# DeltaNet block inversion: turning the inverse in 32x32 blocks on VectorE instead of by TensorE products and a ScalarE copy

## Chip, cores and metric

One core of one Trainium2 chip. The metric is device time in microseconds (us) of one execution, as the median of several runs. TensorE (PE), VectorE (DVE), ScalarE (ACT), GpSimd (POOL) and the DMA queues (SP) run beside each other and meet at semaphores.

## What is computed

A two-layer backbone over 256 context and 256 latent tokens of 1024 channels. Each layer is a half-step SwiGLU feed-forward network, a token mixer, and another half-step feed-forward network; the first mixer is a state-space scan (S5), the second a gated DeltaNet. The change lies in the DeltaNet mixer. For each of 8 heads and 2 scan directions the reference takes chunks of tokens and solves with a unit lower triangular matrix:

```python
decay = jnp.exp(jnp.where(incl, gcum[..., :, None] - gcum[..., None, :], -jnp.inf))
a_mat = jnp.where(strict, jnp.einsum('bhncd,bhnsd->bhncs', k_beta, k) * decay, 0.0)
lhs = a_mat + jnp.eye(GDN_CHUNK, dtype=a_mat.dtype)
u_val = lax.linalg.triangular_solve(lhs, v * beta[..., None], left_side=True, lower=True)
w_key = lax.linalg.triangular_solve(lhs, k_beta * jnp.exp(gcum)[..., None], left_side=True, lower=True)
```

The rest of the mixer (projections, a convolution of five taps over q, k and v, SiLU, norms, the scan over chunks, an output projection) and the networks around it are untouched.

## The kernel before

The tokens are cut into 4 chunks (NCH) of 128, and the kernel forms the inverse of each chunk's triangular matrix, for both directions d = 0, 1. The 128 rows are two halves i of 64 (SUB), which lie on partitions 0 to 63 and 64 to 127. All tiles of the inversion (X, BT, BB, NN) hold 4 chunks of 64 columns for each direction, 128x256 fp32 in all.

`invert(h)` exists three times, for TensorE (line 1747), ScalarE (line 1982) and VectorE (line 2142), each engine walking through the same 10 rounds, in each round first d = 0, then d = 1. After a round's last product TensorE counts up "prod"; VectorE waits for it, evaluates and counts up "evd"; ScalarE, in the rounds listed in `ACT_ROUNDS` (line 1514), copies another bank and counts up "eva". TensorE waits for both before the next round of that direction (lines 1756 to 1758).

- Rounds 0 to 3 build the inverse of the 16x16 diagonal blocks by repeated squaring: X is multiplied up, BB and BT are the power and its transpose. The last addition to X is in round 3 (line 2153).
- Rounds 4 and 5 join pairs of blocks of 16 into blocks of 32, rounds 6 and 7 those of 32 into 64. In round 4 or 6 TensorE turns X by products with an identity (line 1775, 8 products for each direction) and then multiplies NN with half of X's columns (line 1778, 8 products). ScalarE copies the turned X to BT (line 1992), VectorE masks the other product to BB (line 2155). In round 5 or 7 TensorE multiplies BT and BB (line 1783) and VectorE adds the result to half of X's columns (line 2160).
- Rounds 8 and 9 join the two halves of 64 (lines 1785 to 1792, 2162, 2164). Round 8 turns X on half of the partitions and copies it to BT on ScalarE.

Each small product is written through `small`, so the trace has all of them under line 1639; each counts there as two weight loads and two matmuls, and a group of 8 as 16 records. "PS<-consts,X" is a turning product, "PS<-X,NN" the product of round 4 or 6, "PS<-BB,BT" that of round 5, 7 or 9.

Between the rounds the engines also work for the next head. VectorE issues one tap of the next head's key or value convolution (lines 2066, 2069) behind the rounds of `CONV_AFTER` (line 1515): (0,0), (0,1), (1,0), (1,1), (2,0), (3,1), (4,0), (5,1), (6,0), (7,1), written as (round, direction). The last head has none. Each tap but the first waits for the tap before it. ScalarE splits a weight block behind round 2 and runs the SiLU of the next head's keys behind round 4 and of its values behind round 8 (lines 1994 to 1997); the keys' SiLU needs the fifth tap, issued behind (2,0). After round 7 ScalarE copies X to XX (line 2001). Then comes `chain(h)`, the scan over the chunks, with the projection products of head h + 2 (line 1652) put between its steps, and `prepare(h + 1)`.

The order of all of this is the order in which each engine's program is written; there is no planner. All engines' work in this stage is written out, head by head.

```python
            def small(pe, dst, lhsT, rhs, at_row, at_col):

                return pe.matmul(dst, lhsT, rhs, start=True, stop=True, tile_position=(SUB * at_row, SUB * at_col))
```

Of the kernel before, what the change touches and what calls it, by code (L numbers as in the profile page):

```python
# [47 lines left out]
H = 8  # L48
CH = 128
NCH = T // CH  # L50
SUB = CH // 2
# [72 lines left out]
def program(nc, A, out):  # L124

    ctx = ExitStack()
    with ctx:
# [1292 lines left out]
        def glu_pe(pe):  # L1420
# [11 lines left out]
            with pe.Fori(1, KT // 2) as i:  # L1432
# [54 lines left out]

        PER = {"pc": 3, "zr": 1, "conv": 15, "silu": 4, "square": 2, "ss": 1, "norms": 4, "kroot": 1,
# [4 lines left out]
        gs_ = {n: sem("g_" + n) for n in PER}  # L1493
# [17 lines left out]
            ins.then_inc(gs_[name], 1)  # L1511

        ORDER = [(0, 1, 2, 3), (1, 0, 3, 2)]
        ACT_ROUNDS = [0, 1, 2, 4, 6, 8]
        CONV_AFTER = [(0, 0), (0, 1), (1, 0), (1, 1), (2, 0), (3, 1), (4, 0), (5, 1), (6, 0), (7, 1)]
        BESIDE = 2

# [119 lines left out]
        def small(pe, dst, lhsT, rhs, at_row, at_col):  # L1637

            return pe.matmul(dst, lhsT, rhs, start=True, stop=True, tile_position=(SUB * at_row, SUB * at_col))  # L1639
# [17 lines left out]
        def gdn_pe(pe):  # L1657
# [89 lines left out]
            def invert(h):  # L1747
                for rnd in range(10):
                    for d in range(2):
                        banks = ((1, 3, 6), (4, 5, 7))[d]  # L1750
                        if rnd == 0:
                            need(pe, "bt", h, d + 1)
                            need(pe, "bb", h, d + 1)
                            need(pe, "nn", h, d + 1)
                        else:
                            need(pe, "evd", h, 2 * (rnd - 1) + d + 1)
                            if rnd - 1 in ACT_ROUNDS:
                                need(pe, "eva", h, 2 * ACT_ROUNDS.index(rnd - 1) + d + 1)
                            if rnd == 1:
                                need(pe, "x0", h, d + 1)  # L1760
                                if d == 0:
                                    need(pe, "nn", h, 3)
                                else:
                                    need(pe, "kd", h, 2)
                        todo = [[(BB, BT), (BT, BB)], [(BB, X), (BB, BT), (BT, BB)], [(BB, X), (BT, BB)], [(BB, X)]]
                        level = (rnd - 4) // 2
                        if rnd < 4:
                            for (lt, rt), bank in zip(todo[rnd], banks):
                                for c in range(NCH):
                                    for i in range(2):  # L1770
                                        last = small(pe, PS[sub(i), bank, c * SUB:(c + 1) * SUB], lt[sub(i), d, c, :], rt[sub(i), d, c, :], i, i)
                        elif rnd in (4, 6):
                            for c in range(NCH):
                                for i in range(2):
                                    small(pe, PS[sub(i), banks[0], c * SUB:(c + 1) * SUB], X[sub(i), d, c, :], eye_sub[sub(i), :], i, i)
                            for c in range(NCH):
                                for i in range(2):
                                    last = small(pe, PS[sub(i), banks[1], c * SUB // 2:(c + 1) * SUB // 2], NN[sub(i), d, c, :],
                                                 half_columns(X[sub(i), d, c, :], d, level), i, i)
                        elif rnd in (5, 7):  # L1780
                            for c in range(NCH):
                                for i in range(2):
                                    last = small(pe, PS[sub(i), banks[2], c * SUB // 2:(c + 1) * SUB // 2], BT[sub(i), d, c, :],
                                                 BB[sub(i), d, c, 0:SUB // 2], i, i)
                        elif rnd == 8:
                            for c in range(NCH):
                                small(pe, PS[sub(d), banks[0], c * SUB:(c + 1) * SUB], X[sub(d), d, c, :], eye_sub[sub(d), :], d, d)
                                last = small(pe, PS[sub(d), banks[1], c * SUB:(c + 1) * SUB], NNo[sub(1 - d), c, :],
                                             X[sub(1 - d), d, c, :], 1 - d, d)
                        else:  # L1790
                            for c in range(NCH):
                                last = small(pe, PS[sub(d), banks[2], c * SUB:(c + 1) * SUB], BT[sub(d), d, c, :], BB[sub(d), d, c, :], d, d)
                        told(last, "prod")
# [100 lines left out]
        def gdn_act(act):  # L1894
# [87 lines left out]
            def invert(h):  # L1982
                for n, rnd in enumerate(ACT_ROUNDS):
                    for d in range(2):
                        banks = ((1, 3, 6), (4, 5, 7))[d]
                        need(act, "prod", h, 2 * rnd + d + 1)
                        if rnd == 0:
                            need(act, "x0", h, d + 1)
                        copies = {0: [(BT, 0)], 1: [(BT, 1), (BB, 2)], 2: [(BB, 1)]}.get(rnd, [(BT, 0)])
                        rows_ = sub(d) if rnd == 8 else slice(0, P)  # L1990
                        for t, b in copies:
                            last = act.activation(t[rows_, d, :, :].rearrange("p c t -> p (c t)"), PS[rows_, banks[b], 0:NCH * SUB], ACT.Copy)
                        told(last, "eva")
                    if rnd == 2 and h + 1 < H:
                        split_half(1, u0 + h + 2, 0)
                    if rnd in (4, 8) and h + 1 < H:
                        silu(h + 1, (rnd - 4) // 4)
                for d in range(2):
                    need(act, "evd", h, 15 + d)
                    for i in range(2):  # L2000
                        last = act.activation(XX[sub(i), d, :, sub(i)], X[sub(i), d, :, :], ACT.Copy)
                    told(last, "xx")
# [50 lines left out]
        def gdn_dve(dve):  # L2053
# [88 lines left out]
            def invert(h):  # L2142
                ahead = list(conv_steps(h + 1))[:10] if h + 1 < H else []
                for rnd in range(10):
                    for d in range(2):
                        banks = ((1, 3, 6), (4, 5, 7))[d]
                        level = (rnd - 4) // 2
                        need(dve, "prod", h, 2 * rnd + d + 1)
                        if rnd == 0:
                            last = dve.tensor_copy(BB[:, d, :, :].rearrange("p c t -> p (c t)"), PS[:, banks[1], 0:NCH * SUB])  # L2150
                        elif rnd < 4:
                            xd = X[:, d, :, :].rearrange("p c t -> p (c t)")
                            last = dve.tensor_tensor(xd, xd, PS[:, banks[0], 0:NCH * SUB], ALU.add)
                        elif rnd in (4, 6):
                            last = dve.tensor_tensor(BB[:, d, :, 0:SUB // 2],
                                                     PS[:, banks[1], 0:NCH * SUB // 2].rearrange("p (c t) -> p c t", c=NCH),
                                                     join(level, d).unsqueeze(1).to_broadcast([P, NCH, SUB // 2]), ALU.mult)
                        elif rnd in (5, 7):
                            xd = half_columns(X[:, d, :, :].rearrange("p c t -> p (c t)"), d, level)
                            last = dve.tensor_tensor(xd, xd, PS[:, banks[2], 0:NCH * SUB // 2].rearrange("p (b j) -> p b j", j=C16 << level), ALU.add)  # L2160
                        elif rnd == 8:
                            last = dve.tensor_copy(BB[sub(d), d, :, :].rearrange("p c t -> p (c t)"), PS[sub(d), banks[1], 0:NCH * SUB])
                        else:
                            last = dve.tensor_copy(XX[sub(d), d, :, sub(1 - d)],
                                                   PS[sub(d), banks[2], 0:NCH * SUB].rearrange("p (c t) -> p c t", c=NCH))
                        told(last, "evd")
                        if ahead and (rnd, d) in CONV_AFTER:
                            conv(h + 1, *ahead.pop(0))

# [370 lines left out]
```

## Time and profile before

| | |
|---|---|
| median of 3 runs | 2112.87 us (2112.18 to 2113.4) |
| the profiled execution, its own time | 2116.53 us |
| its span, first to last instruction | 2114.7 us |
| mean granted TensorE clock | 0.971 |
| TensorE busy | 1974.8 us, 93% |
| TensorE weight loads | 1671.6 us, 79% |
| VectorE busy | 1482.6 us, 70% |
| ScalarE busy | 707.2 us, 33% |
| GpSimd busy | 589.1 us, 28% |

Busy time is the time in which at least one instruction of the engine runs. Matmuls overlap, so a busy TensorE isn't TensorE at its peak. The DeltaNet heads lie between about 1500 and 1856 us of the span. A line of the trace names the source line, the operation, the tile written, the tiles read, and the shape; the bracket at its end is idle time of that engine just before it, and who ended it. Times on the left of a timeline count from the span's start.

### The profile page before, as it was taken

To read this page: it belongs to the slowest core of one execution; us is meant where nothing else is said; L and a number is where in the kernel's file an instruction comes from. 1 tells how busy PE (TensorE), PEld (TensorE's weight loads), DVE (VectorE), ACT (ScalarE), POOL (GpSimd) and SP (SyncE) were. 2 spreads that over 40 slices of the span, in tenths; PEclk is the share of its full clock that TensorE was granted. 3 is DMA by queue.
4 is the path that set the end of the run, shared out by engine and by line. 5 is a ranking of instruction groups with operands and counts; after the bars stand their busy time and mean duration, and the time that the engine had idled before them with its cause. 6 is when DMAs were issued, how large, how long until landed. Compare 5 with 4: busy or idle time off the path is not lost.

```text
span 2114.7 us, 37558 instructions
## 1 busy us (share of the span) xinstructions
PE 1974.8 (93%) x14838; PEld 1671.6 (79%) x14838; DVE 1482.6 (70%) x2273; ACT 707.2 (33%) x1126; POOL 589.1 (28%) x465
## 2 busy tenths in 40 slices
PE   3999999997998999999989999998999999879997
PEld 0778778776986788888768888886888998779996
DVE  8968768757735985858989486358577777655555
ACT  2322222224333421222243122225455555426332
POOL 2245575553922120212412021140000000022113
PEclk8999999998999999999999999998999999989999
DMA  8365665655734354644425353222111111014553
GB/s 324 130 243 197 202 223 202 211 178 204 295 120 138 120 179 139 216 142 154 175 100 192 135 178 139 95 85 64 42 45 50 50 42 61 23 60 161 179 178 98
DMA packets 85633, 305.04 MB, mean 144 GB/s; under 512 B 9856, under 2 KB 21632, under 8 KB 76032
## 3 DMA queue, kind: packets, MB, share of 16 engines
q1 hardware_dynamic: 80896, 285.41, 39.5%
q0 software_dynamic: 2304, 9.44, 1.1%
q10 hardware_dynamic: 2304, 8.39, 1.0%
q8 instruction: 92, 1.51, 0.3%
q14 instruction: 37, 0.30, 0.0%
HBM read 275.94 MB, written 27.26 MB: 143 GB/s over the span
## 4 chain that ended last, share of the span: by engine, by line
PE 82%; DVE 9%; ACT 3%; issue 2%; POOL 2%; DVEq 1%; DMA 1%; SPq 0%; ACTq 0%; POOLq 0%
PE PS L228 41%; PE PS L219 6%; PE PS L221 6%; PE PS L220 6%; PE PS L1639 6%; PE PS L1652 6%; PE PS L1236 1%; DVE wlo L264 1%; PE PS L620 1%; DVE rstd L386 1%; PE PS L1071 1%; POOL hidl L603 1%; PE PS L1198 1%; PE PS L1218 1%; PE PS L1045 1%
## 5 line engine op out<-in xcount | busy, mean ns | idle before, releaser
L264 DVE TENSOR_TENSOR wlo<-raw,whi 128x1024 fp32r<-128x1024 f32 x314 | 479.0, 1566 | 80.9 <-ACT whi L258 79.2
L228 PE MATMUL PS<-hh,whi 128*128 128x512 f32 (+1 forms) x1536 | 443.9, 371 | 37.2 <-DVE hl L407 30.0
L228 PE MATMUL PS<-hl,whi 128*128 128x512 f32 (+1 forms) x1536 | 440.1, 368 | 0.0
L228 PE MATMUL PS<-hh,wlo 128*128 128x512 f32 (+1 forms) x1536 | 439.3, 368 | 0.0
L258 ACT ACTIVATE whi<-raw 128x1024 fp32r<-128x1024 f32 x300 | 301.3, 1052 | 277.6 <-PE PS L221 246.0
L228 PEld LDWEIGHTS PS<-hh,whi 128*128 128x128 f32 x1536 | 278.0, 191 | 92.4 <-issue 37.6
L228 PEld LDWEIGHTS PS<-hl,whi 128*128 128x128 f32 x1536 | 280.3, 191 | 47.2
L228 PEld LDWEIGHTS PS<-hh,wlo 128*128 128x128 f32 x1536 | 280.2, 191 | 47.1
L601 POOL CAST hidh<-gt 128x512 f32 (+2 forms) x88 | 62.0, 704 | 860.7 <-DVE gt L549 860.7
L219 PE MATMUL PS<-hidh,whi 128*128 128x512 f32 (+1 forms) x704 | 259.3, 368 | 12.7 <-POOL hidl L603 10.0
L221 PE MATMUL PS<-hidh,wlo 128*128 128x512 f32 (+1 forms) x704 | 256.6, 365 | 0.0
L220 PE MATMUL PS<-hidl,whi 128*128 128x512 f32 (+1 forms) x704 | 256.6, 364 | 0.0
L520 ACT ACTIVATE gt<-PS 128x512 f32<-128x512 f32 (+1 forms) x88 | 47.9, 544 | 570.8 <-PE PS L228 570.7
L649 DVE CUSTOM_DVE_ANT_0 junk<-modw,cb,modb 128x1024 f32<-128x1024 f32 x160 | 216.9, 1356 | 4.3
L586 DVE SCALAR_TENSOR_TENSOR x<-PS,hg,x 128x256 f32<-128x256 f32 (+1 forms) x176 | 77.9, 478 | 154.6 <-PE PS L221 152.0
L219 PEld LDWEIGHTS PS<-hidh,whi 128*128 128x128 f32 x704 | 133.7, 190 | 37.9 <-POOL hidl L603 12.7
L603 POOL TENSOR_TENSOR hidl<-gt,hidh 128x512 f32 (+2 forms) x88 | 157.6, 1791 | 12.6 <-POOL hidh L601 10.8
L549 DVE TENSOR_TENSOR gt<-gt,PS 128x512 f32<-128x512 f32 (+1 forms) x88 | 54.7, 621 | 138.4 <-ACT gt L520 135.5
L221 PEld LDWEIGHTS PS<-hidh,wlo 128*128 128x128 f32 x704 | 133.5, 190 | 21.0
L220 PEld LDWEIGHTS PS<-hidl,whi 128*128 128x128 f32 x704 | 133.7, 190 | 20.1
L2279 POOL TENSOR_TENSOR X<-BT,consts 128x256 f32<-128x256 f32 x16 | 13.6, 847 | 344.6 <-DVE BT L2122 344.6
L1652 PE MATMUL PS<-hh,whi 128*128 128x512 f32 (+1 forms) x256 | 72.6, 366 | 7.8 <-DVE hl L407 7.6
(336 smaller groups left out, 2755.5 us busy)
## 6 DMA issues: line engine op xcount, KB each, us to landing
modw<-in_mod_w SPq DMA_DIRECT2D x72, 1024.0 KB, 5.0
raw<-in_w_gdn SPq DMA_DIRECT2D x32, 512.0 KB, 4.1
cxd<-cx POOLq DMA_DIRECT2D x16, 576.0 KB, 3.8
cxS<-cxd SPq DMA_DIRECT2D x8, 1152.0 KB, 6.2
raw<-in_w_f0p0a SPq DMA_DIRECT2D x16, 512.0 KB, 6.9
vwd<-vws ACTq DMA_DIRECT2D x16, 512.0 KB, 6.5
raw<-in_w_f0p1a SPq DMA_DIRECT2D x16, 512.0 KB, 5.6
raw<-in_w_glu SPq DMA_DIRECT2D x16, 512.0 KB, 4.6
```

The costliest lines, as they stand in the source:

```text
L219: pe.matmul(dst, w_h, xh, start=first, stop=False)
L220: pe.matmul(dst, w_h, xl, start=False, stop=False)
L221: return pe.matmul(dst, w_l, xh, start=False, stop=last)
L228: ended = pe.matmul(dst, of[:, slot, c:c + P], moving, start=first and part_ == 0, stop=last and part_ == 2)
L258: act.activation(whi[:, s, c], raw[:, s, c], ACT.Copy).then_inc(whi_ready[half][s], 1)
L264: dve.tensor_tensor(wlo[:, s, c], raw[:, s, c], whi[:, s, c].bitcast(F32), ALU.subtract)\
L586: last = dve.scalar_tensor_tensor(out=xv, in0=pv, scalar=hg[:, layer, n, bass.ds(dt, 1), w:w + 1].rearrange("p a b -> p (a b)"), in1=xv, o ...
L601: pool.tensor_copy(hidh[:, bass.ds(2 * i + s, 1), c0:T], gt[:, s:s + 1, c0:T]).then_inc(hidh_ready[s], 1)
L603: pool.tensor_tensor(hidl[:, bass.ds(2 * i + s, 1), c0:T], gt[:, s:s + 1, c0:T], hidh[:, bass.ds(2 * i + s, 1), c0:T].bitcast(F32), ALU.su ...
L649: dve.tensor_tensor_reduce(out=junk[:, :], in0=modw[:, k % MS, D * j:D * j + D], in1=cb[:, w, :], scale=1.0, scalar=modb[:, layer, a:a + 1 ...
L1639: return pe.matmul(dst, lhsT, rhs, start=True, stop=True, tile_position=(SUB * at_row, SUB * at_col))
L1652: last = pe.matmul(PS[:, 2 * s + i, 0:T - c0], (whi, whi, wlo)[part_][:, s, (2 * k + i) * P:(2 * k + i + 1) * P], (hh, hl, hh)[part_][:, k ...
```

## The change

Rounds 4 and 6 lose their turning products on TensorE and their copies to BT on ScalarE. Behind its additions to X in rounds 3 and 5 VectorE waits for its own result and then turns each 32x32 block of X[:, d] in place of the block, into BT. Round 8 keeps its products and its copy. ScalarE's rounds become 0, 1, 2 and 8, and the SiLU of the next head's keys moves from behind round 4 to behind round 2. The number of "eva" counts of a head drops from 12 to 8.

```diff
-               "ntT": 3, "nn": 3, "bt": 2, "bb": 2, "x0": 2, "xx": 2, "prod": 20, "eva": 12, "evd": 20, "RS": 6, "qS": 4, "r2": 6,
+               "ntT": 3, "nn": 3, "bt": 2, "bb": 2, "x0": 2, "xx": 2, "prod": 20, "eva": 8, "evd": 20, "RS": 6, "qS": 4, "r2": 6,
...
-        ACT_ROUNDS = [0, 1, 2, 4, 6, 8]
+        ACT_ROUNDS = [0, 1, 2, 8]
...
                         elif rnd in (4, 6):
                             for c in range(NCH):
                                 for i in range(2):
-                                    small(pe, PS[sub(i), banks[0], c * SUB:(c + 1) * SUB], X[sub(i), d, c, :], eye_sub[sub(i), :], i, i)
-                            for c in range(NCH):
-                                for i in range(2):
                                     last = small(pe, PS[sub(i), banks[1], c * SUB // 2:(c + 1) * SUB // 2], NN[sub(i), d, c, :],
                                                  half_columns(X[sub(i), d, c, :], d, level), i, i)
...
-                    if rnd in (4, 8) and h + 1 < H:
-                        silu(h + 1, (rnd - 4) // 4)
+                    if rnd in (2, 8) and h + 1 < H:
+                        silu(h + 1, rnd // 8)
...
                         told(last, "evd")
+                        if rnd in (3, 5):
+                            need(dve, "evd", h, 2 * rnd + d + 1)
+                            dve.transpose(BT[:, d, :, :].rearrange("p c t -> p (c t)"), X[:, d, :, :].rearrange("p c t -> p (c t)"))
                         if ahead and (rnd, d) in CONV_AFTER:
                             conv(h + 1, *ahead.pop(0))
```

## Rows read from the trace of the kernel before

**Rows 1.** The page, part 4: shares of the chain that ended last, by engine.

```profile
PE 82%; DVE 9%; ACT 3%; issue 2%; POOL 2%; DVEq 1%; DMA 1%; SPq 0%; ACTq 0%; POOLq 0%
```

**Rows 2.** Stretches: from:to, length, busy us (x records) by engine, clock, DMA.

```profile
1489.40:1494.20 4.80, 2.89 (x23) 2.46 (x23) 4.21 (x16) 4.72 (x11) 0.68 (x1) 1.00 0.00 0
1494.50:1497.50 3.00, 3.00 (x26) 2.67 (x25) 2.37 (x6) 2.75 (x8) 0.73 (x1) 0.50 0.02 5
1553.10:1571.30 18.20, 16.23 (x497) 15.59 (x496) 13.38 (x31) 8.80 (x19) 1.12 (x2) 1.00 0.19 62
1571.30:1602.00 30.70, 30.52 (x242) 27.41 (x240) 23.30 (x64) 16.77 (x43) 1.70 (x2) 1.00 0.11 35
1835.60:1839.00 3.40, 3.40 (x71) 3.40 (x68) 1.04 (x3) 0.77 (x2) 1.12 (x2) 0.50 0.02 5
```

**Rows 3.** Timeline of TensorE's weight loads, head 1, rounds 3 to 9 (start, length).

```profile
1562.04 0.54 PEld L1639 LDWEIGHTS PS<-X,BB 64*64 64x64 f32 x16 [0.24 <-DVE X L2153]
1562.50 0.55 PEld L1639 LDWEIGHTS PS<-consts,X 64*64 64x64 f32 x16
...
1564.36 0.55 PEld L1639 LDWEIGHTS PS<-BB,BT 64*64 64x64 f32 x16
1565.10 0.57 PEld L1639 LDWEIGHTS PS<-BB,BT 64*64 64x64 f32 x16 [0.19 <-DVE BB L2155]
...
1568.19 0.48 PEld L1639 LDWEIGHTS PS<-BB,BT 64*64 64x64 f32 x13 [0.18 <-DVE BB L2155]
...
1570.24 1.00 PEld L1639 LDWEIGHTS PS<-BB,BT 64*64 64x64 f32 x16 [0.44 <-DVE BB L2162]
```

**Rows 4.** Timeline of VectorE, head 1, rounds 2 to 8.

```profile
1561.57 0.82 DVE L2153 TENSOR_TENSOR X<-X,PS 128x256 f32<-128x256 f32 x2
1562.77 0.42 DVE L2153 TENSOR_TENSOR X<-X,PS 128x256 f32<-128x256 f32 x1 [0.38 <-PE PS L1639]
1563.11 0.48 DVE L2066 TENSOR_SCALAR cv<-pv,convw 128x512 f32<-128x512 f32 x1
1563.67 0.29 DVE L2155 TENSOR_TENSOR BB<-PS,consts 128x128 f32<-128x128 f32 x1
1563.88 0.74 DVE L2069 SCALAR_TENSOR_TENSOR cv<-pv,convw,cv 128x512 f32<-128x512 f32 x1
1564.61 0.29 DVE L2155 TENSOR_TENSOR BB<-PS,consts 128x128 f32<-128x128 f32 x1
1565.07 0.29 DVE L2160 TENSOR_TENSOR X<-X,PS 128x128 f32<-128x128 f32 x1 [0.17 <-PE PS L1639]
...
1568.91 0.29 DVE L2160 TENSOR_TENSOR X<-X,PS 128x128 f32<-128x128 f32 x1 [0.47 <-PE PS L1639]
...
1569.78 0.87 DVE L2162 COPY BB<-PS 64x256 f32<-64x256 f32 x2
```

**Rows 5.** Timeline of VectorE, four taps in a row, each waiting for the last.

```profile
1461.21 3.12 DVE L2069 SCALAR_TENSOR_TENSOR ck<-pk,convw,ck 128x512 f32<-128x512 f32 x4
```

**Rows 6.** Timeline of ScalarE, head 1, round 4.

```profile
1564.61 0.38 ACT L1992 ACTIVATE BT<-PS 128x256 f32<-128x256 f32 x1 [0.55 <-PE PS L1639]
1565.01 1.28 ACT L1926 ACT_TABLE_LOAD   x1
```

**Rows 7.** Groups by line and shape in the DeltaNet stage: one group of VectorE.

```profile
L2212 DVE TENSOR_TENSOR oo<-oo 128x256 f32<-128x256 f32 x7 | 3.0, 425 | 0.2
```

**Rows 8.** Timeline of VectorE, head 0: X(3,1) and BB(8,0).

```profile
1513.89 0.42 DVE L2153 TENSOR_TENSOR X<-X,PS 128x256 f32<-128x256 f32 x1 [0.36 <-PE PS L1639]
...
1520.90 0.87 DVE L2162 COPY BB<-PS 64x256 f32<-64x256 f32 x2
```

**Rows 9.** Timeline of VectorE, head 7: X(3,1) and BB(8,0).

```profile
1844.29 0.42 DVE L2153 TENSOR_TENSOR X<-X,PS 128x256 f32<-128x256 f32 x1 [0.36 <-PE PS L1639]
...
1850.91 0.42 DVE L2162 COPY BB<-PS 64x256 f32<-64x256 f32 x1 [0.18 <-PE PS L1639]
```

**Rows 10.** Waits of TensorE from 1500 to 1856 us: total, times, longest.

```profile
PE PS L1639 <- issue: 6.0, 7, 1.3
```

## Prediction

> **What bounds the kernel now.** I read the page's last chain first, to see which engine sets the end; then stretches of one head of the DeltaNet stage, to see whether that holds inside the inversion; then the instructions of TensorE and VectorE there, one by one, because the change moves work between these two. In the chain of the whole run TensorE has 82% and VectorE 9% [rows 1], so TensorE's work normally counts in full. In head 1 the scan after the inversion is TensorE without a hole: 30.52 us busy of 30.70. The inversion before it is not: 16.23 of 18.20, with VectorE busy for 13.38 [rows 2]. Ten rounds go back and forth between the two, with the two directions of the scan taking turns to hide the way.
>
> **The marks of head 1** [rows 3, 4]. A group of 8 small products (16 records) starts 0.47 us after the one before (1562.04, 1562.50). VectorE starts on its result 0.71 to 0.73 us after the group's start (1564.36 to 1565.07, 1562.04 to 1562.77). TensorE starts 0.05 after the end of the VectorE result it waits for (X of round 2 ends at 1561.99, group at 1562.04). On VectorE an instruction that waits for nothing starts 0.08 before its predecessor's end (1562.77 + 0.42 = 1563.19, next at 1563.11). One that waits for its predecessor's own result starts later: four taps in a row take 3.12 us, at 0.74 each 0.79 from start to start, so 0.045 after the end [rows 5, 4].
>
> **What goes from TensorE.** Rounds 4 and 6 lose the transposing products, one group of 0.47 us for each of two directions: 4 groups, 1.87 us a head, 14.9 us in 8 heads. ScalarE loses four copies a head. Of these, the one at 1564.61 ends at 1564.99, later than VectorE's 1564.90, and the group starts at 1565.10 instead of 1564.95 [rows 3, 4, 6]: 0.15 us of waiting that goes, twice a head (round 5 and round 7).
>
> **What comes to VectorE.** After the additions into X of rounds 3 and 5, for each direction, one transposition of 128x256 fp32, with a wait for X's own end: 4 a head, 32 in all. The trace has none. The nearest rows are one pass over 256 columns: 0.42 from SBUF to SBUF [rows 7] and 0.42 with PSUM [rows 4]. The lower bound is the 0.29 of a pass over 128 columns, the upper the 0.74 of one over 512 (as if it needed two passes) [rows 4]. I take 0.42: same columns, type and memory. They cannot save anything by themselves; that is in the TensorE terms.
>
> **The walk through a head, at 0.42.** A tap of the next head's convolution still stands behind each odd round's second direction and each even round's first, and it is now queued behind the transpositions too.
> - X(3,0) (round 3, direction 0) ends at 1562.39; its transposition takes 1562.44 to 1562.86. X(3,1) may start at 1562.77, starts at 1562.78, ends at 1563.20. Nearly free: it fills the 0.38 of idle before it.
> - Transposition 1563.24 to 1563.66, tap to 1564.06, BB(4,0) 1563.98 to 1564.27 (was 1563.67): TensorE needed it at 1564.36 and now starts round 5 at 1564.32. So the products removed bought 0.04 there.
> - Tap to 1564.93, BB(4,1) 1564.85 to 1565.14; round 5's second group at 1565.19, was 1565.10.
> - X(5,0) 1565.06 to 1565.35, transposition to 1565.82; X(5,1) waits for its product: 1565.92 to 1566.21 (0.18 of slack). Transposition to 1566.67, tap to 1567.33, BB(6,0) 1567.25 to 1567.54, tap to 1568.20, BB(6,1) 1568.12 to 1568.41. Round 7 starts at 1567.59, and its second group at 1568.46, was 1568.19.
> - X(7,1) 1569.19 to 1569.48 (was 1568.91), tap to 1570.15, BB(8,0) at 1570.07, was 1569.78. Round 9 waits for that, was 1570.24, now 1570.53.
>
> So a head with taps gets 0.29 us **longer**: 1.87 us leave TensorE, and VectorE's queue, 2.2 us longer (4 x 0.42 and four waits of 0.125), is what is late next. From X(3,1) to BB(8,0) there are 7.01 us in head 1 and in head 0 [rows 4, 8]; heads 2 to 6 run the same instructions in the same order: 7 x 0.29 = +2.0 us. Head 7 has no taps; there the distance is 6.62 [rows 9]. The same walk from 1844.29 without them puts X(7,1) at 1849.05 and BB(8,0) at about 1849.64 instead of 1850.91: -1.3 us. **Sum: +0.7 us.** What follows (ScalarE's copies of X into XX, the scan) hangs on the same marks and moves along.
>
> One more look at the wait. The Trainium skill ("VectorE: DVE Perf Modes", The DRAIN you can't avoid) says that semaphores between chained VectorE operations cost nothing extra. By that, two of the 0.125 us on the path would go, and the sum would be about -1.0 us. The taps' 0.79 against a step of 0.34 without such a wait speaks against it.
>
> **Costed at nothing.** The SiLU of the keys moves on ScalarE from behind round 4 to behind round 2. Its table load of 1.28 [rows 6] and the SiLU, under 1 us, now lie where ScalarE has no copy until round 8, some 4 us later; without that cover it would be up to 2.3 us a head. Its input is the fifth tap, which is issued in round 2. No DMA and no other queue is touched. TensorE's waits for "issue" in these products, 6.0 us in 7 places [rows 10], may move, since the stream loses instructions and those behind get other places: between 0 of them and twice as many, -6 to +6. I take 0.
>
> **Rivals.**
> - **A: TensorE stays the bound, faster.** If VectorE's additions fell in its idle time, all of the 14.9 us would come: 2112.9 - 14.9 = 2098. For it: VectorE is idle 4.8 us of the 18.20 [rows 2]. Against: the idle time lies before round 3's second half and in rounds 0 to 2, not behind the taps, where the queue is closed from 1563.24 to 1565.35. A milder form: the issue waits shrink by over 5 us, giving 2108.
> - **B: the block transposition is slow, slower.** Three of the four lie in the closed queue and the fourth has 0.18 of slack. Each 0.1 us more costs 0.3 us a head, above 0.60 it costs 0.4. From about 0.57 us the kernel is slower by over 0.2%; at 0.74 a head costs 1.4 us: +10 us, 2123.
> - **C: TensorE's clock falls, slower.** The granted clock fell to half (1.2 of 2.4 GHz) after a stretch with 2.89 us busy of 4.80, and at half clock 71 small products take 3.40 us, 0.77 a group instead of 0.47 [rows 2, 3]. The walk leaves TensorE about 55% issuing in rounds 5 to 7. If it falls late in the inversion, the scan begins at half clock: with about 1.7 us of it there, and two groups that take 0.3 longer, 2.3 us a head, +16 us, 2129. Against: TensorE's wait of 1.3 us among these products [rows 10] left the clock at 1.00 in head 1. The Trainium skill ("TensorE: Matmul & The Clock Gate", A second HAM failure mode) says that small idle gaps between groups of products can make the clock swing to and fro; head 1, with clock 1.00 at 16.23 of 18.20 busy, doesn't show it.
> - **D: it doesn't do what it says.** X is zero outside its 16 or 32 wide diagonal blocks at both places, so turning each 32x32 block in place is the transpose. The products really go. I give it nothing.
>
> **Chances.** No change (within 0.2%, or 4.2 us, about what a measurement of this kernel can tell) 0.5; A in either form 0.2; B 0.12; C 0.18. Together: faster 0.2, same 0.5, slower 0.3. The profiled execution took 2116.53 us, 3.66 above the median 2112.87; I add the sum to the median: **2113.6 us**. The range from 2107 (lowest price 0.29, worth 2.1 us, and most of the issue waits) to 2126 (B whole, half of C) leaves out A's full form and C's upper part.
>
> **What would show it.** Right: 32 transpositions of 0.40 to 0.46; round 5 and 7's second groups waiting for VectorE's BB; TensorE's busy time down by some 14 us and its idle time up as much; X(3,1) to BB(8,0) 7.3 us in heads 0 to 6 and 5.3 in head 7; clock 1.00 there. Wrong: that distance at about 5.1 in heads 0 to 6 (A), transpositions over 0.57 (B), a clock of 0.5 in any of heads 1 to 6 (C), or issue waits of TensorE that add up to 3 us more or less than 6.

## The result and the profile after

The changed kernel takes **2134.45 us** (2127.25 to 2136.71 in 4 runs), the kernel before 2112.52 (2111.57 to 2113.40, 4 runs): ratio 1.0102, interval 1.0086 to 1.0118. It is slower by some 22 us, where 2113.6 was forecast and the range ended at 2126. What came about is the forecast's rival C, at a higher price than it was given there: TensorE's clock falls to half in every head.

The profiled execution took 2136.15 us, its span is 2134.3. The page after, parts 1 and 4:

```profile
PE 1991.0 (93%) x14326; PEld 1682.2 (79%) x14326; DVE 1490.4 (70%) x2305; ACT 695.0 (33%) x1094; POOL 589.8 (28%) x465
...
PE 81%; DVE 10%; ACT 3%; POOL 2%; issue 2%; DVEq 1%; DMA 1%; SPq 0%; ACTq 0%; POOLq 0%
```

This page alone misleads. TensorE has 512 records fewer (14326, before 14838), so the products really went, and yet it is busy 16.2 us **longer** (1991.0, before 1974.8); the chain shares are those of [rows 1] to within one point. Fewer products and more busy time: each must have become slower on average. The stretches of the DeltaNet stage show why. Columns as in [rows 2]; the value after POOL's is the granted clock:

```profile
1500.00:1800.00 300.00, 287.31 (x3929) 260.94 (x3928) 216.96 (x554) 138.41 (x326) 14.12 (x20) 0.90 0.13 42
1516.70:1526.90 10.20, 10.06 (x94) 8.86 (x95) 4.18 (x11) 3.87 (x9) 0.00 (x0) 0.50 0.01 2
1567.90:1578.10 10.20, 10.20 (x95) 9.00 (x94) 3.84 (x10) 3.87 (x9) 0.00 (x0) 0.50 0.01 2
1823.90:1834.10 10.20, 9.90 (x108) 8.63 (x106) 6.04 (x16) 3.87 (x9) 0.00 (x0) 0.50 0.01 2
1578.10:1602.00 23.90, 23.90 (x187) 21.65 (x186) 18.64 (x54) 13.55 (x34) 1.70 (x2) 1.00 0.15 46
```

Before, the clock is 1.00 throughout 1500 to 1800 us. After, it is at half (1.2 of 2.4 GHz) for 10.2 us in each of heads 0 to 6, seven times, beginning some 51.2 us apart (1516.7, 1567.9, ... 1823.9). Two stretches of 6.8 us follow, in head 6's scan (from 1844.3) and in head 7 (from 1868.2); before, that part has two of 3.4 us, one of them in [rows 2]. The timeline of TensorE's weight loads shows where in head 1 the first slow one lies:

```profile
1562.66 0.58 PEld L1639 LDWEIGHTS PS<-X,NN 64*64 64x64 f32 x16
1563.43 0.55 PEld L1639 LDWEIGHTS PS<-X,NN 64*64 64x64 f32 x16 [0.19 <-DVE X L2150]
1564.48 0.54 PEld L1639 LDWEIGHTS PS<-BB,BT 64*64 64x64 f32 x16 [0.50 <-DVE BB L2152]
1565.34 0.55 PEld L1639 LDWEIGHTS PS<-BB,BT 64*64 64x64 f32 x16 [0.32 <-DVE BB L2152]
1565.80 1.13 PEld L1639 LDWEIGHTS PS<-X,NN 64*64 64x64 f32 x32
1567.70 1.69 PEld L1639 LDWEIGHTS PS<-BB,BT 64*64 64x64 f32 x30 [0.77 <-DVE BB L2152]
1571.07 1.53 PEld L1639 LDWEIGHTS PS<-BB,BT 64*64 64x64 f32 x16
1574.16 0.76 PEld L1652 LDWEIGHTS PS<-hh,whi 128*128 128x128 f32 x2
...
1578.58 0.30 PEld L1652 LDWEIGHTS PS<-hl,whi 128*128 128x128 f32 x2
```

In rounds 3 to 7 the loads now stand apart by 0.50, 0.32 and 0.77 us, each time behind VectorE's BB, where [rows 3] had 0.19 and 0.18. That is the forecast's picture (VectorE's queue is late, TensorE waits). But the third wait is the last at full clock: at 1567.9, in round 7, the clock falls, and round 7's two groups, rounds 8 and 9 and the beginning of the scan run at half of it. Two weight loads of the projection take 0.76 us there and 0.30 behind 1578.1. In heads 2, 3, 5 and 6 the clock falls earlier, in round 6 and ahead of the third wait (in head 2 at 1619.1, with round 7 starting at 1620.3 after a wait of only 0.38), so the wait of 0.77 isn't needed to bring it down. VectorE in the same head:

```profile
1562.63 0.45 DVE L2166 STREAM_TRANSPOSE BT<-X 128x256 f32<-128x256 f32 x1
1563.00 0.38 DVE L2150 TENSOR_TENSOR X<-X,PS 128x256 f32<-128x256 f32 x1
1563.41 0.45 DVE L2166 STREAM_TRANSPOSE BT<-X 128x256 f32<-128x256 f32 x1
1563.78 0.45 DVE L2063 TENSOR_SCALAR cv<-pv,convw 128x512 f32<-128x512 f32 x1
1564.14 0.28 DVE L2152 TENSOR_TENSOR BB<-PS,consts 128x128 f32<-128x128 f32 x1
1564.34 0.74 DVE L2066 SCALAR_TENSOR_TENSOR cv<-pv,convw,cv 128x512 f32<-128x512 f32 x1
1565.00 0.28 DVE L2152 TENSOR_TENSOR BB<-PS,consts 128x128 f32<-128x128 f32 x1
1565.20 0.28 DVE L2157 TENSOR_TENSOR X<-X,PS 128x128 f32<-128x128 f32 x1
1565.52 0.45 DVE L2166 STREAM_TRANSPOSE BT<-X 128x256 f32<-128x256 f32 x1
...
1567.36 0.28 DVE L2152 TENSOR_TENSOR BB<-PS,consts 128x128 f32<-128x128 f32 x1
1568.22 0.28 DVE L2152 TENSOR_TENSOR BB<-PS,consts 128x128 f32<-128x128 f32 x1
1569.67 0.29 DVE L2157 TENSOR_TENSOR X<-X,PS 128x128 f32<-128x128 f32 x1 [0.60 <-PE PS L1639]
1570.58 0.42 DVE L2159 COPY BB<-PS 64x256 f32<-64x256 f32 x1
```

**Where the time went.** From X(3,1) to BB(8,0) head 1 takes 7.58 us (1563.00 to 1570.58), before 7.01 [rows 4]: +0.57, of which the forecast had 0.29. From BB(8,0) to the next head's first mark (the BB copy of round 0) it takes 36.41 us (to 1606.99), before 33.39 (1569.78 to 1603.17): +3.02, in a part in which no instruction was changed. In the other heads 0 to 5 this part is 2.4 to 2.8 us longer. Seven head periods together (first mark of head 0 to that of head 7) grew from 330.4 to 353.2 us, +22.8 or 3.25 a head; 3.1 come back before the first mark (1.7) and behind the last one (1.4). 22.8 - 3.1 is, to rounding, the difference of the two profiled executions (2136.15 - 2116.53 = 19.6).

### The profile page after: what moved, and what is told of

It reads as the page before. It is cut to its first block, busy times and chain, and to the rows that moved or that the text cites. A ratio compares the mean times of both kernels' runs of the same rounds, so it can differ in the third digit from the quotient of the medians.

```text
span 2134.3 us, 36502 instructions
## 1 busy us (share of the span) xinstructions
PE 1991.0 (93%) x14326; PEld 1682.2 (79%) x14326; DVE 1490.4 (70%) x2305; ACT 695.0 (33%) x1094; POOL 589.8 (28%) x465
## 4 chain that ended last, share of the span: by engine, by line
PE 81%; DVE 10%; ACT 3%; POOL 2%; issue 2%; DVEq 1%; DMA 1%; SPq 0%; ACTq 0%; POOLq 0%
PE PS L228 40%; PE PS L219 6%; PE PS L1652 6%; PE PS L221 6%; PE PS L220 6%; PE PS L1639 6%; DVE wlo L264 1%; PE PS L1236 1%; PE PS L620 1%; DVE rstd L386 1%; PE PS L1071 1%; POOL hidl L603 1%; PE PS L1847 1%; PE PS L1045 1%; DVE cv L2066 1%
```

## The experiments

Theory at this point: the clock costs the time, and it falls because TensorE's issue has become thinner (products gone and waits on VectorE). Rivals: VectorE's longer queue by itself, the moved SiLU with its table load, the transposition. Times are medians, but a trace shows one execution: those of e1 (2107.15 us), e4 (2104.42) and e9 (2098.52) are 4 us faster than the medians, those of e6 (2128.03) and e12 (2112.74) 7.5 and 4 us slower. The number of falls of the clock that is read from a trace is that of this one execution.

### The products come back (e1), the SiLU alone (e2)

e1 is the changed kernel with the turning products of rounds 4 and 6 computed again, into the bank they had; nothing reads them.

```diff
+                            for c in range(NCH):
+                                for i in range(2):
+                                    small(pe, PS[sub(i), banks[0], c * SUB:(c + 1) * SUB], X[sub(i), d, c, :], eye_sub[sub(i), :], i, i)
```

> The changed kernel, with the transposing products of rounds 4 and 6 kept on TensorE (nothing reads their result; VectorE still turns X). Clock theory (the 20 us come from TensorE's granted clock, which falls in each head because TensorE idles behind VectorE's late BB in rounds 5 to 7): the products fill that idle time, the clock stays at 1.00 through heads 1 to 6, and VectorE's longer queue alone is left, about 0.35 us a head with taps: 2112.5 + 2.5 = 2115, between 2113 and 2118. Queue theory (the four turns and their waits on VectorE cost about 3 us a head by themselves): nothing is taken off VectorE, so 2134 or more. ScalarE theory (the SiLU moved behind round 2 delays something): 2134.

Measured: 2111.33 us, 1.0001 (0.9991 to 1.0010) of the kernel before. The stretch:

```profile
1500.00:1790.00 290.00, 282.76 (x4488) 260.11 (x4485) 228.36 (x586) 145.77 (x344) 16.95 (x24) 1.00 0.14 47
```

TensorE's waits in that stage (total, times, longest):

```profile
PE PS L1639 <- DVE BB L2155: 1.4, 7, 0.2
```

The clock is 1.00 again, and the waits for BB are 1.4 us in 7 places, instead of 7.2 in 21 in the changed kernel. So 14.9 us of work that nobody needs makes the changed kernel some 22 us faster. VectorE's four transpositions, their waits and the moved SiLU are all in e1 and cost nothing that the whole time shows; in head 1 they are worth 0.14 us, as X(3,1) to BB(8,0) takes 7.15 us (before 7.01).

e2 is the kernel before with the keys' SiLU moved as the change moves it.

```diff
-                    if rnd in (4, 8) and h + 1 < H:
-                        silu(h + 1, (rnd - 4) // 4)
+                    if rnd in (2, 8) and h + 1 < H:
+                        silu(h + 1, rnd // 8)
```

> The kernel before, with only the SiLU of the next head's keys moved on ScalarE from behind round 4 to behind round 2. Clock theory and queue theory: the move lies in ScalarE's idle time, 2112.5 within 1.5. ScalarE theory: most of the 20 us, 2125 to 2134.

Measured: 2114.53, 1.0013 (1.0001 to 1.0025), clock 1.00 up to 1790 us. The move alone is worth some 2.7 us, by the interval 0.2 to 5.3, and so can't be the 22.

### Without the transpositions (e3)

```diff
-                        if rnd in (3, 5):
-                            need(dve, "evd", h, 2 * rnd + d + 1)
-                            dve.transpose(...)
```

> The changed kernel without the four VectorE transpositions of a head and without their waits, so BT holds round 1's value in rounds 5 and 7 and the inverse is left incomplete; TensorE's products are still gone. Queue theory: the queue is even shorter than before the change, so the time is under that of before: by my walk -0.65 us in a head with taps and -1.3 in the last, 2106. Clock theory: it depends on whether TensorE's idle time of about 1.2 us a head is enough without the turns: if the clock stays at 1.00 in heads 1 to 6, 2106 too; if it falls, over 2120 although nothing at all was added to VectorE.

Measured: 2118.97, 1.0037 (1.0023 to 1.0051), for a kernel whose inverse is left incomplete, as nothing turns X in rounds 4 and 6.

```profile
1500.00:1790.00 290.00, 281.75 (x3967) 255.92 (x3967) 209.41 (x545) 142.76 (x340) 14.32 (x21) 0.94 0.14 45
```

Here TensorE has 15 us less to do than before and VectorE nothing more, and the kernel is still slower: the clock is 0.94 (at half in five stretches of 6.8 or 10.2 us here, and in two more behind it). A slow transposition (B) can't be the cause. With e1 this makes a pair: adding work to TensorE mends the time, taking work from VectorE mends only some of it.

### VectorE's queue cleared in rounds 3 to 6 (e4)

Four taps move out of rounds 3 to 6, where the transpositions are, to rounds 7 to 9, and the SiLU of the values, which needs the last tap, behind the XX copies.

```diff
-        CONV_AFTER = [..., (2, 0), (3, 1), (4, 0), (5, 1), (6, 0), (7, 1)]
+        CONV_AFTER = [..., (2, 0), (7, 0), (7, 1), (8, 1), (9, 0), (9, 1)]
```

> The changed kernel with the four taps behind (3,1), (4,0), (5,1), (6,0) moved behind (7,0), (8,1), (9,0), (9,1), and the SiLU of the values moved behind ScalarE's copies into XX. The turns stay. VectorE's queue in rounds 3 to 7 then is that of head 7. Queue theory: the distance from X(3,1) to BB(8,0) falls from 7.6 to about 6 us and the kernel is faster than before, about 2103. Clock theory: it is that fast only if the clock stays at 1.00 through heads 1 to 6 (TensorE's idle time there shrinks by about 1.5 us a head); if it still falls for 10 us a head, about 2122.

Measured: 2108.47, 0.9984 (0.9974 to 0.9993).

```profile
1500.00:1790.00 290.00, 284.43 (x4170) 259.01 (x4171) 230.78 (x588) 146.91 (x348) 16.94 (x24) 0.97 0.15 49
```

In a head in which the clock stays up, X(3,1) to BB(8,0) takes 5.61 us, 1.4 less than before: that is rival A's mechanism, and it needed only the taps out of the way. But the clock still falls in two heads of this stretch (heads 1 and 3, at 1559.5 and 1655.1, for 6.8 and 10.2 us) and again in head 6 (1798.5, 6.8 us). This one trace also prices the clock: from BB(8,0) to the next head's first mark the heads without a fall (0, 2, 4, 5) take 33.40 or 33.41 us, head 1 takes 35.14 and head 3 takes 36.31, with the same instructions.

### Half of the products (e5, e6), other filling (e7, e8)

e5 keeps the turning products in round 4 alone, e6 in round 6 alone (e1's lines under `if rnd == 4` or `if rnd == 6`).

> The changed kernel with the transposing products kept in round 4 alone (result unread); those of round 6 are gone. Half of what the first experiment put back. Clock theory: the time follows how long the clock is at half in the DeltaNet heads. The changed kernel has 72 us of that in heads 0 to 6 for 20 us, so 0.28 us for each: 2112 plus 0.28 times what this trace shows, somewhere between 2112 and 2130. Queue theory has no reason for any time under 2130, as VectorE's work is the same.

> The same with the products kept in round 6 alone. The longest idle time of TensorE in the changed kernel is before round 7 (0.77 us), so I expect this half to hold the clock better than round 4's: nearer to 2112 than the other, again 0.28 us for each us at half clock.

Measured: e5 2125.80, 1.0058 (1.0042 to 1.0075), with stretches of 6.8 us at half clock in all of heads 0 to 6; e6 2120.50, 1.0039 (1.0025 to 1.0053), none in heads 0 and 1, 10.2 us in each of heads 2 to 6. The stage's clock is 0.93 in both; e5's row:

```profile
1500.00:1800.00 300.00, 289.74 (x4190) 263.83 (x4188) 221.72 (x572) 143.62 (x340) 15.61 (x22) 0.93 0.14 44
```

Half the work brings back 9 and 14 of the 22 us.

e7 and e8 fill with useful work: eight 128x512 projection products of head h + 2, one behind each group of rounds 4 to 7, taken from those that stand between the scan's steps. e7 has e4's taps besides, e8 has those of the changed kernel.

```diff
+                        n = {(4, 0): 1, (4, 1): 1, ..., (7, 1): 1}.get((rnd, d), 0)
+                        if n and h + 2 < H:
+                            if h + 2 not in ahead_of:
+                                need(pe, "at", h, 3)
+                            ahead_some(h + 2, n)
```

> The kernel with the taps late, with useful work in TensorE's gaps: one 512 column product of the projection for head h + 2 (the bank 0 half, which no round uses) behind each group of rounds 4 to 7, 8 a head in heads 0 to 5, taken out of the scan that follows. Clock theory: clock at 1.00 through heads 1 to 5, and each of these heads gets back up to the 1.87 us that its products gave: 2111.5 - 6 x 1.7 = 2101, between 2099 and 2106. If idle time is not what makes the clock fall, the falls of the taps-late kernel (6.8 and 10.2 us in two of heads 1 to 5) stay and so does its time, 2108.

> The changed kernel, taps where they were, with the same 8 projection products a head in rounds 4 to 7. VectorE's queue is as in the change. Clock theory: no falls in heads 1 to 5, and the 1.84 us of useful work fill what VectorE's queue leaves idle (0.3 us a head are lost to the queue): 2111.5 - 6 x 1.5 = 2102.5, plus some 3 us for head 6, which has no projection left to fill with: 2103 to 2108. Queue theory: 2130 or more.

Measured: e7 2108.82, 0.9984 (0.9973 to 0.9995); e8 2110.19, 0.9988 (0.9978 to 0.9998). The clock is 1.00 up to 1790 us in both, as expected; the times miss, e7's by 8 us. The weight loads of e8 show what eats the gain:

```profile
1557.23 0.58 PEld L1639 LDWEIGHTS PS<-X,NN 64*64 64x64 f32 x16
1557.85 0.19 PEld L1695 LDWEIGHTS PS<-hh,whi 128*128 128x128 f32 x1
1558.28 0.55 PEld L1639 LDWEIGHTS PS<-X,NN 64*64 64x64 f32 x16 [0.24 <-issue]
```

From the start of the first small group to that of the second there are 1.05 us, where two groups back to back are 0.47 apart [rows 3]. So one 128-row product among 64-row ones takes 0.58 us there, though its own load is 0.19: the load starts 0.15 late (at 1557.85 instead of 1557.70), and behind it are 0.24 us for which no semaphore is named. These holes of 0.39 us among the weight loads lie at 8 places in each of six heads. Part of them falls into waits for VectorE. What they cost can be read from e7 beside e4's heads without a fall: X(3,1) to BB(8,0) takes 8.57 us instead of 5.61, and the part behind it 31.70 instead of 33.40, since the eight products are gone from it. That is 1.26 us a head, 0.16 a place, and 7.6 us in six heads, about e7's miss of 8. Why the array needs the holes was not tried.

### Spread small filling (e9, e12) and its controls (e10, e11)

e9 is e4 with four small products behind each group of rounds 4 and 6, into the unused bank: half of what the change removed, but in both rounds and both directions.

```diff
+                        if rnd in (4, 6):
+                            for c in range(2):
+                                for i in range(2):
+                                    small(pe, PS[sub(i), banks[0], c * SUB:(c + 1) * SUB], X[sub(i), d, c, :], eye_sub[sub(i), :], i, i)
```

> The kernel with the taps late, with half of the removed products put back as pure filler: 4 of 8, result unread, behind the real products of each direction in rounds 4 and 6, after the count that VectorE waits for, so they run while TensorE would wait. Clock theory: in the taps-late kernel an inversion without a fall is 5.6 us from X(3,1) to BB(8,0) instead of 7.0, but three of its heads fell to half clock. The filler lies in 1 us of idle time a head, costs at most 0.3 us a head, and keeps the clock at 1.00 in heads 0 to 6: 2111.5 - 8 x 1.2 = 2102, between 2100 and 2105, faster than both kernels. If the falls are chance and not idle time, they stay and the time is 2108 or more.

Measured: **2102.74** (2098.52 to 2105.12, 6 runs), 0.9958 (0.9946 to 0.9970): faster than both kernels. X(3,1) to BB(8,0) takes 5.75 us in head 1, and the clock holds in heads 0 to 5; it falls once in head 6, for 10.2 us from 1810.3. The stretch of heads 0 to 5:

```profile
1500.00:1790.00 290.00, 283.33 (x4497) 261.00 (x4492) 235.59 (x600) 150.17 (x352) 16.94 (x24) 1.00 0.15 47
```

The small filling has no such holes around it, unlike e8's (weight loads, head 0):

```profile
1506.70 0.58 PEld L1639 LDWEIGHTS PS<-X,NN 64*64 64x64 f32 x16
1507.17 0.34 PEld L1639 LDWEIGHTS PS<-consts,X 64*64 64x64 f32 x8
1507.47 0.54 PEld L1639 LDWEIGHTS PS<-X,NN 64*64 64x64 f32 x16
1507.93 0.32 PEld L1639 LDWEIGHTS PS<-consts,X 64*64 64x64 f32 x8
1508.17 1.02 PEld L1639 LDWEIGHTS PS<-BB,BT 64*64 64x64 f32 x32
```

e10 is e4 with the useful products in two places only, three behind (4,1) and three behind (6,1), to pay for fewer changes of shape.

```diff
+                        n = {(4, 1): 3, (6, 1): 3}.get((rnd, d), 0)
```

> The kernel with the taps late and useful filler, but in two places instead of eight: three 512 column projection products behind (4,1) and three behind (6,1). The kernel with eight places lost its gain to the change between products of 64 rows and of 128: the next group starts 0.43 us after the filler's weight load, and the group before takes 0.62 instead of 0.47, so about 0.3 us a place, 2.6 us a head. With two places that is 0.7 us a head against 1.4 us of work moved into idle time: 2111.5 - 6 x 1.6 - 1 = 2101, between 2099 and 2105, clock 1.00 in heads 1 to 5. If the changeover is not what ate the gain, 2108 as with eight places.

Measured: 2105.56, 0.9964 (0.9951 to 0.9977). Its median is 3 us under e7's, though the clock falls from 1795 us on, in three stretches of 10.2, 13.7 and 6.8 us. X(3,1) to BB(8,0) takes 7.26 us and the part behind it 32.16 in head 1: 0.4 us a head over e4's heads without a fall, where e7 lost 1.26. Fewer places cost less, as expected.

e11 asks whether late taps alone are the gain: the kernel before with e4's edits of the taps and of the values' SiLU.

> The control for the best version: the kernel before, all products and ScalarE's copies in place, with only the taps late and the SiLU of the values behind the copies into XX. If the best version's 9 us come from the products that are gone, this one shows only the small waits for VectorE before round 3's and round 9's groups: TensorE issues without a gap in rounds 4 to 7 anyway, so 2112.5 within 3, at best 2109. If the taps alone are what counts, it is at 2103 too.

Measured: 2112.54, 1.0001 (0.9993 to 1.0010), clock 1.00 up to 1790 us. The late taps are worth nothing while the products are there: X(3,1) to BB(8,0) takes 7.01 us in head 1, as before.

e12 is the changed kernel with e9's filling alone, taps as they are.

> The changed kernel, taps where they were, with the same half of the products put back as filler as in the best version. Clock theory: the filler takes 0.9 of the 2.2 us a head in which TensorE idles; the experiments with the products of one round kept had as much work and still fell (20 to 34 us short of none), so some falls stay: 2113 to 2122, at 0.28 us for each us at half clock. Without any fall it would be 2111.5 + 7 x 0.1 to 0.3 - 1 = 2112. Queue theory: 2130.

Measured: 2108.91, 0.9983 (0.9973 to 0.9993), which is below the expected span of 2113 to 2122 us: the clock falls in no head up to 1790.

```profile
1500.00:1790.00 290.00, 279.70 (x4233) 255.57 (x4232) 226.44 (x584) 145.49 (x343) 15.82 (x22) 1.00 0.14 46
```

e5, e6 and e12 add the same number of products to the changed kernel, 16 a head (0.93 us), and take 2125.8, 2120.5 and 2108.9. So not only how much TensorE issues counts, but where. The place differs in two ways, which no run takes apart: e12 spreads the products over both rounds, and it puts them behind the real products, where TensorE would wait, while e5 and e6 have them ahead, as the kernel before had. The waits for BB in the weight loads show the difference, e12 in head 1 first, then e5 and e6 in head 2:

```profile
1561.57 0.54 PEld L1639 LDWEIGHTS PS<-BB,BT 64*64 64x64 f32 x16 [0.27 <-DVE BB L2156]
1562.42 0.54 PEld L1639 LDWEIGHTS PS<-BB,BT 64*64 64x64 f32 x16 [0.32 <-DVE BB L2156]
...
1564.78 0.55 PEld L1639 LDWEIGHTS PS<-BB,BT 64*64 64x64 f32 x16 [0.41 <-DVE BB L2156]
```

```profile
1617.30 0.54 PEld L1639 LDWEIGHTS PS<-BB,BT 64*64 64x64 f32 x16 [0.77 <-DVE BB L2156]
```

```profile
1608.87 0.54 PEld L1639 LDWEIGHTS PS<-BB,BT 64*64 64x64 f32 x16 [0.50 <-DVE BB L2156]
```

e5 keeps the wait of 0.77 us ahead of round 7, e6 that of 0.50 ahead of round 5, and the clock falls; in e12's head 1 no wait for BB is over 0.41, and it doesn't. But the longest wait is not the rule: in e3 none of these waits is over 0.32, and the clock falls in heads 0 to 4; in e4 the longest idle time named in rounds 3 to 7 is 0.21, and it falls in heads 1 and 3; e6's first two heads have the waits of the others (0.50 and 0.32) and escape. What decides in a single head stays open.

## Why the prediction was wrong

The step that failed is the one that let the scan "move along": the forecast carried the marks of the inversion into a scan at full clock, and gave the other outcome, C, 0.18. In its place the runs show the clock at half for 10.2 us in each of heads 0 to 6, from late in the inversion on, and a scan and what follows that take 36.41 us in head 1 instead of 33.39.

- **The walk through a head was right up to the fall.** Shifted by the 0.22 us by which X(3,1) stands later in the trace after, the forecast has BB(4,0) at 1564.20, BB(4,1) at 1565.07, BB(6,0) at 1567.47 and BB(6,1) at 1568.34; measured are 1564.14, 1565.00, 1567.36 and 1568.22, up to 0.12 early. X(7,1) was due at 1569.41 and came at 1569.67, as round 7 already ran at half clock.
- **Transposition:** taken at 0.42, measured 0.445, 32 of them (minimum, median and maximum of one in ns: 444/445/446):

```profile
L2166 DVE STREAM_TRANSPOSE BT<-X x32: 444/445/446, 1511.8 to 1866.6; 128x256 f32<-128x256 f32 x32
```

  Rival B falls with it. The wait for X's own result was about right: the transposition starts 0.03 to 0.04 behind the end of X (1563.38 to 1563.41, 1565.48 to 1565.52), where an instruction that waits for nothing starts 0.08 before it. That makes 0.11 to 0.12 beside the 0.125 taken. By the Trainium skill ("VectorE: DVE Perf Modes", The DRAIN you can't avoid) a semaphore between chained operations costs nothing extra; here it costs these 0.11 to 0.12 us.
- **Issue waits of TensorE:** taken at no change, and so they were: 6.2 us in 7 places, before 6.0 in 7 [rows 10]. TensorE's waits after, 1500 to 1880 us:

```profile
PE PS L1639 <- DVE BB L2152: 7.2, 21, 0.7
PE PS L1639 <- issue: 6.2, 7, 1.4
```

- **ScalarE's SiLU at nothing:** e2's interval leaves 0.2 to 5.3 us (the ratios 1.0001 and 1.0025 of 2111.53), but e1, which has the move as well, stands at 1.0001. Right within what can be told.
- **TensorE's waits on BB** came where the walk has them, ahead of the groups of round 5 and of round 7. **Its busy time** was to fall by some 14 us and rose by 16.2: the sign that the forecast named for C (a clock of 0.5 in heads 1 to 6) decides it.
- **Head 7** was to take 5.3 us from X(3,1) to BB(8,0), 1.3 less than before. It took 5.9 (1863.80 to 1869.69, before 6.62 [rows 9]): the clock falls there too, at 1868.2. In e4's trace the same head, with the same instructions and no fall, takes 5.22.
- **Rival A** was blocked by the taps, as the forecast argued. e4 shows most of it come about once they are moved: 5.61 us in a head without a fall, where A in full would be 5.1.
- **Rival C** was right in mechanism and place (late in the inversion, the scan begins at half clock) and under-sized twice. Its price: 2.3 us a head were taken, from about 1.7 us of clock lost in the scan and two slower groups; measured were 3.25, since the clock stayed down for 10.2 us. (The "71 small products" of its working are 71 records, two to a product; its 0.77 a group of 16 records is right.) In head 1, +3.0 of it lie in the scan and what follows (1.7 taken) and +0.57 in the inversion (0.29 for the queue, 0.3 for the groups: +0.59 taken). Seven times 3.25 is 22.8; by the profiled executions the total is 19.6 and by the medians 22, instead of 16.
- **Its chance** was the real miss. It rested on one counterexample, a wait of 1.3 us in head 1 that left the clock at 1.00. But that wait lies by itself in an inversion that is otherwise dense; the changed kernel has three smaller waits, 0.50, 0.32 and 0.77, between groups of about 0.5 to 1.1 us. One long hole in dense work was no evidence on several short ones in thin work. The row that was nearer to it spoke for C: the clock at half behind a stretch with 2.89 us busy of 4.80 [rows 2], beside the forecast's own "55% issuing in rounds 5 to 7". Here the trace now agrees with the Trainium skill ("TensorE: Matmul & The Clock Gate", A second HAM failure mode), which reports for a kernel with bf16 products of 512 columns that small idle gaps between groups make the clock swing: here it goes down and up again once a head. I had set this rule aside because the kernel *before* didn't show it, though it was that kernel's dense products that the change takes away.

The cause itself is shown: e1 gives the products back and with them the clock and all of the time, e12 does it with half of them, e7 and e8 do it with other products, and e2 and e3 exclude the SiLU and the transposition as its source. That the part between BB(8,0) and the next head is longer through the clock alone is shown by e1 too, which has 33.38 us there (before 33.39, after 36.41), and by e4, where it is 33.40 in heads without a fall and 35.14 and 36.31 in the two with one. Not shown is which property of TensorE's work in these rounds makes the clock fall.

## What to carry to other kernels

Where work is taken from TensorE in a part that leaves it waiting, and a dense stage follows, look first at the granted clock of every stretch: here 14.9 us of products removed cost 22 us, and busy time went up with fewer instructions. Here the change paid with two things beside it: the other engine's side work moved out of the exchange, and a little filling of the same product shape, put into the waits of both rounds. Either alone gave 2108.5 and 2108.9 us, both together 2102.7 against 2112.6, with half of the removed work put back. Test a fear of the clock on the stretch most like the new one, not on the longest wait found elsewhere.

## What the runs showed that I had not expected

- Half clock came in stretches of 10.2 us a head in the changed kernel, and 3.25 us were lost in each head; dense scan work at half clock didn't bring it back sooner (1567.9 to 1578.1 is busy for 10.20 of 10.20 us). In e5 the stretches are 6.8 us.
- The same 0.93 us of filling a head gives 2125.8, 2120.5 or 2108.9 us by where it lies (e5, e6, e12), in which rounds and ahead of or behind the real products.
- Less work on TensorE and ScalarE with none added on VectorE is slower (e3, +7.4 us), and unread work on TensorE makes it faster (e1 against the changed kernel, some 22 us).
- A 128-row product between groups of 64-row ones brings holes of 0.39 us with it (e8), so useful filling of another shape (e7, 2108.8) lost to unread filling of the same one (e9, 2102.7).
